# Post norms by column sums, shift products inside their wait, the last additions on TensorE, and five smaller reorderings, in a 512-token transformer stack

## What is computed

```python
# block 1
x = x + mixed @ w_out              # mixed: gated mLSTM branch and gated differential attention branch
x = x + ffn_conv(rmsnorm(x))       # up 1024->2*2816, conv over 3 tokens, gelu gate, down
x = x + sigmoid(rmsnorm(x) @ w_ple_gate) * (p @ w_ple)
# block 2: two layers
x = x + (stick_breaking(...) * silu(gate)) @ w_out
x = x + (mla(...)            * silu(gate)) @ w_out      # 8 heads, 4 query blocks of 128 each
# block 3
for sub in (swiglu, hybrid_mixer, swiglu):              # each with shift, scale, gate from w_ada
    h = sub(rms_norm(x, g_pre) * (1 + scale) + shift)
    x = x + c * (1 + gate) * rms_norm(h, g_post)        # the POST NORM of this document; c = 0.5, 1, 0.5
# hybrid_mixer holds the forgetting ("FoX") attention: 8 heads, logits = q k / 8 + cum[q] - cum[k]
```

## Time and profile before

| | |
|---|---|
| median of 3 runs | 2669.25 us (2667.76 to 2672.13) |
| the profiled execution | 2670.79 us, of which the span is 2669.0 us |
| TensorE busy | 2469.7 us, 93% of the span |
| VectorE, ScalarE, GpSimd busy | 51%, 38%, 38% |
| mean granted TensorE clock | 0.964 |
| HBM traffic | 242.06 MB read, 91 GB/s over the span |

### The profile page before, as it was taken

How to read it: one execution, slowest core, us unless ns; L and a number is a source line. 1 busy time by engine, 2 the same in 40 slices (tenths; PEclk the granted TensorE clock), 3 DMA queues, 4 the chain that set the end, 5 groups by cost and what they waited for, 6 DMA issues and landing times.

```text
span 2669.0 us, 31132 instructions
## 1 busy us (share of the span) xinstructions
PE 2469.7 (93%) x11612; PEld 1976.9 (74%) x11612; DVE 1362.1 (51%) x1883; ACT 1022.4 (38%) x1320; POOL 1013.0 (38%) x758
## 2 busy tenths in 40 slices
PE   6999799899998999998988899999979997899996
PEld 5887677688887778676766678888859655688885
DVE  6456567866667561444447652222373535522225
ACT  4444476422223444665456442222242433322221
POOL 3332244455444443122433244444424104344442
PEclk8999899999999999999999899999989998999998
DMA  3220497222222121111221122222222001122221
GB/s 135 80 79 32 166 359 271 103 95 94 95 98 90 68 91 64 48 48 48 91 83 64 48 79 95 94 94 94 94 69 94 32 17 63 63 95 99 102 98 47
DMA packets 35812, 245.50 MB, mean 92 GB/s; under 512 B 3935, under 2 KB 3935, under 8 KB 7044
## 3 DMA queue, kind: packets, MB, share of 16 engines
q1 hardware_dynamic: 29952, 207.12, 21.7%
q10 hardware_dynamic: 5764, 37.06, 3.7%
HBM read 242.06 MB, written 2.11 MB: 91 GB/s over the span
## 4 chain that ended last, share of the span: by engine, by line
issue 56%; POOL 27%; PE 14%; DVE 2%; DVEq 1%; POOLq 0%; ACT 0%; ACTq 0%
POOL WL L280 27%; PE PS L310 5%; PE PS L312 5%; PE PS L311 5%; DVE ARENA L2350 0%; DVE X L2355 0%; DVE ARENA L1683 0%; POOLq L284 0%; DVEq L2354 0%; DVE ARENA L1701 0%; DVEq L2031 0%; DVE ARENA L1708 0%; DVEq L1724 0%; PE PS L372 0%; POOLq L277 0%
## 5 line engine op out<-in xcount | busy, mean ns | idle before, releaser
L280 POOL TENSOR_TENSOR WL<-WT,WH 128x512 fp32r<-128x512 f32 x754 | 1012.8, 1374 | 1617.0 <-ACT WH L1012 1097.7
L310 PE MATMUL PS<-HH,WH 128*128 128x512 f32 x1568 | 623.5, 398 | 30.7 <-DVE HL L1717 8.8
L312 PE MATMUL PS<-HH,WL 128*128 128x512 f32 x1568 | 615.8, 393 | 0.0
L311 PE MATMUL PS<-HL,WH 128*128 128x512 f32 x1568 | 615.6, 393 | 0.0
L1334 ACT CAST WH<-WT 128x2048 fp32r<-128x2048 f32 x90 | 172.1, 1912 | 604.1 <-PE PS L310 604.1
L310 PEld LDWEIGHTS PS<-HH,WH 128*128 128x128 f32 x1568 | 297.6, 190 | 109.3 <-DVE HL L1717 14.2
L310 PE MATMUL PS<-YH,WH 128*128 128x512 f32 x840 | 337.4, 402 | 41.5 <-POOL WL L280 8.7
L312 PEld LDWEIGHTS PS<-HH,WL 128*128 128x128 f32 x1568 | 297.4, 190 | 63.2
L311 PEld LDWEIGHTS PS<-HL,WH 128*128 128x128 f32 x1568 | 297.9, 190 | 59.6 <-issue 0.3
L311 PE MATMUL PS<-YL,WH 128*128 128x512 f32 x840 | 332.2, 395 | 0.0
L312 PE MATMUL PS<-YH,WL 128*128 128x512 f32 x840 | 332.2, 395 | 0.0
(11 more groups left out here) (290 smaller groups left out, 3354.2 us busy)
## 6 DMA issues: line engine op xcount, KB each, us to landing
WT<-weights SPq DMA_DIRECT2D x188, 1024.0 KB, 4.9
ARENA<-w_ada ACTq DMA_DIRECT2D x33, 1024.0 KB, 7.3
ARENA<-w_ada SPq DMA_DIRECT2D x3, 1024.0 KB, 7.6
X<-x_fm SPq DMA_DIRECT2D x4, 512.0 KB, 8.0
out_fm<-X SPq DMA_DIRECT2D x8, 256.0 KB, 2.0
ARENA<-rel_rows ACTq DMA_DIRECT2D x1, 1024.0 KB, 5.2
CON<-constants SPq DMA_DIRECT2D x1, 704.0 KB, 10.1
WT<-weights SPq DMA_DIRECT2D x1, 512.0 KB, 5.5
```

Source lines behind the costliest of these rows:

```text
L280: i = nc.gpsimd.tensor_tensor(WL[s][:, e], WT[s][:, e], WH[s][:, e].bitcast(F32), ALU.subtract)
L310: i0 = nc.tensor.matmul(o, w[0], r[0], start=first, stop=False, skip_group_check=True)
L311: nc.tensor.matmul(o, w[0], r[1], start=False, stop=False, skip_group_check=True)
L312: i2 = nc.tensor.matmul(o, w[1], r[0], start=False, stop=last, skip_group_check=True)
```

## The change

1. **Post norms.** `norm_sum(two_parts)` is replaced by `post_sum`: the sum over features is taken with the squares as the stationary operand and one column of ones as the moving one, so it comes out as 128 x 4 (token within a block on the partition, block in the column). DVE adds up only the squares 0 to 4; the parts 5, 6 and 7 go to TensorE one by one. ACT's root and DVE's reciprocal are then of 128 x 4 elements. DVE writes four diagonal blocks (identity times factor, 128 x 512) and one float32 matmul with ONES spreads them over the partitions in bank 5, from where L2350's successor reads the factor.
2. **Inside the wait.** The next panel's first shift products stand between the column sums and that matmul. ACT casts the next panel right behind the root instead of after the third tile of `raw_after_post`. Eight matmuls of no use (`keep_warm`) stand ahead of the raw tile. A `sqrt_ahead` (a function table load) stands ahead of the squares in both later FFNs.
3. **Last post norm.** X[0] to X[4] are added on TensorE: identity times X[k], then identity times the scaled ACC[k], both float32 in one bank; ACT copies the sum to X[k]. DVE adds 5 to 7 as before.
4. **Merge.** The sum for the last head of differential attention stands behind the first tile of panel `G_MERGE`; SP loads panel `G_MERGE + 2` ahead of the wait for `da_done`.
5. **FFN1's end.** ACT's copies of PLE tiles 0, 1, 2 stand behind the raw tiles 5, 6, 7.
6. **MLA.** `OUT3_STEPS` goes; the first output panel is computed whole after the last tile.
7. **FoX.** The decay is added by one matmul of 128 rows: the high part in rows 0 to 7, the low part in rows 32 to 39 of `LBH`, the stationary operand picks both.

```diff
-            def norm_sum(second=False, two_parts=False):
+            def post_sum(bank, meanwhile):
                 n["sq"] += DT
-                n["acc"] += DT - 2 if two_parts else DT - 1
+                n["acc"] += POST_ACC
...
+                for k in range(POST_ACC, DT):
+                    if k > POST_ACC:
+                        pe.wait_ge(sem("sq_ready"), n["sq"] - DT + k + 1)
+                    part = SQ[:, (k - 1) % 3, :] if k > POST_ACC else ACC1
+                    for t in range(NQ):
+                        m = nc.tensor.matmul(PS[:, bank + t, 0:1], part[:, P * t:P * (t + 1)], ONES[:, 0:1], start=k == POST_ACC,
+                                             stop=k == DT - 1, skip_group_check=True)
+                m.then_inc(sem("ms_ready"), 1)
+                meanwhile()
+                pe.wait_ge(sem("diag_ready"), n["post"])
+                nc.tensor.matmul(psb(5), ONES, NRS, start=True, stop=True).then_inc(sem("nrow_ready"), 1)
...
-            norm_sum(two_parts=True)
+            post_sum(2, lambda: shift_ahead(G_FFN3, 2))
             ffn(G_FFN3, sums="tiles", shift=2)
-            norm_sum(two_parts=True)
...
+            post_sum(0, lambda: (last_add(0, X), last_add(1, X)))
+            for k in range(LAST):
+                if k + 2 < LAST:
+                    last_add(k + 2, X)
+                pe.wait_ge(sem("last_norm"), k + 1)
+                last_add(k, ACC)
...
+            def post_root(bank):
+                act.wait_ge(sem("ms_ready"), n["ms"])
+                f(COLS[:, 40:44], PS[:, bank:bank + NQ, 0], ACT.Sqrt, scale=1.0 / D, bias=par("eps")).then_inc(sem("root_ready"), 1)
...
+            def post_factor():
...
+                nc.vector.reciprocal(COLS[:, 44:48], COLS[:, 40:44])
+                dve.drain()
+                tt(NRS.rearrange("p (t n) -> p t n", t=NQ), IDENT.unsqueeze(1).to_broadcast([P, NQ, P]),
+                   COLS[:, 44:48].unsqueeze(2).to_broadcast([P, NQ, P]), ALU.mult).then_inc(sem("diag_ready"), 1)
...
-                        stt(out=NT[:, k % 3, :], in0=ACC[:, k, :], scalar=mod(s, 2)(k), in1=NRS, op0=ALU.mult, op1=ALU.mult)
+                        stt(out=NT[:, k % 3, :], in0=ACC[:, k, :], scalar=mod(s, 2)(k), in1=psb(5), op0=ALU.mult, op1=ALU.mult)
...
-            stream(2, G_MERGE + 2)
+            stream(2, G_MERGE + 3)
             sp.wait_ge(sem("da_done"), 1)
...
-            da_squares(DA_HEADS - 1)
+            open_panel(G_MERGE)
+            feature_tiles(G_MERGE, G_MERGE % 2, 8, 256, h_hi, h_lo, (0,))
+            pe.wait_ge(sem("dsq_ready"), DA_HEADS)
+            nc.tensor.matmul(psb(2), ONES, SQB_, start=True, stop=True).then_inc(sem("dsum_ready"), 1)
+            feature_tiles(G_MERGE, G_MERGE % 2, 8, 256, h_hi, h_lo, (P,), first_of_panel=False)
...
-                one = CONR[0:8, COFF["ident"] + w:COFF["ident"] + w + 1].to_broadcast([8, P])
-                for part in (LBH, LBL):
-                    nc.tensor.matmul(o, one, part[0:8, k], start=False, stop=False, skip_group_check=True)
+                nc.tensor.matmul(o, LBH[:, S + w:S + w + 1].to_broadcast([P, P]), LBH[:, k], start=False, stop=False,
+                                 skip_group_check=True)
...
                 if conv:
-                    raw(lambda k: par("norm_ple", k))
+                    for k in range(DT):
+                        raw(lambda k: par("norm_ple", k), k, k + 1)
+                        if k >= 5:
+                            embed(k - 5)
```

More of the change, by code:

```diff
@@ L368, in norm_sum @@
                 pe.wait_ge(sem("sq_acc"), n["acc"])
[L369 to L372 removed]
+                m = nc.tensor.matmul(psb(3), ONES, ACC1, start=True, stop=True)
                 m.then_inc(sem("ms_ready"), 1)
@@ L434, in out_gemm, with keep_warm @@
                         i2.then_inc(sem("a_done"), 1)
+            def keep_warm(o, count):
+                for _ in range(count):
+                    nc.tensor.matmul(o, IDENT_R, CONR[:, 0:S], start=True, stop=True, skip_group_check=True)
             def out_step(g, src, ready, c, b, k):
@@ L1735, in trail @@
                     raw_lo(k, gain, dst)
[L1736 removed]
+                if gain or k <= POST_ACC:
                     accumulate(k)
```

165 lines of the change are left out of this document (99 added, 66 removed).

## The result

The changed kernel takes 2635.91 us (median of four runs, 2633.1 to 2638.14) beside 2670.69 for the kernel before (four runs, 2667.76 to 2674.76): a ratio of 0.9865, 95% interval 0.9851 to 0.9879. 35 us are gone.

A forecast was written before the change was run, and what follows sets the result against it. TensorE, busy 93% of the span, was taken as the bound, so removed matmuls or idle time count. Terms 4.5 + 8.4 + 4.5 + 4.0 + 5.0 + 7.5 = 33.9 us off 2670.79 give 2636.9, 2635 beside the median; range 2625 to 2648.

The forecast's parts named there:

- A: Rival: clock and GpSimd overlap decide, the post norms gain 1 us instead of 12.9, giving 2647 us; chance 0.12.
- B: Rival: merge and MLA reorderings only move holes, gaining 1 us instead of 9.5, giving 2644 us; chance 0.13.
- D: Rival: FoX's granted clock falls to 1.2 GHz and the kernel is slower, 2745 us at half clock throughout; chance 0.03.
- FoX, 7.5 predicted: FoX's decay: one matmul fewer per tile, mean 0.24 us over 32 tiles, 7.5 us saved after some waits.
- Merge, 4.5 predicted: Merge stage: third panel ready near 315 us instead of 318.53, perhaps fewer slow matmuls; 4.5 us saved, between 0 and 6.
- which is 3.1 later: Merge stage: ACT waits for `CROW` only, which comes 3.1 us later, so the third panel's cast starts at 307.4.
- FFN1's end, 4.0 predicted: End of FFN1: earlier copies move the chain of copies, cast and GpSimd's pieces by 4.0 us, at least 2.
- MLA, 5 predicted: MLA's output: steps leave the tiles, two holes and nine half-clock matmuls go; 5 us saved, between 0 and 9.
- The two post norms, 4.2 each predicted: After FFN2 and the mixer: 2.4 us from an earlier factor plus 1.8 from GpSimd's overlap, each between 1.5 and 6.
- the column sums of the last part are four matmuls ... so 0.96: Post norms: behind the last square only four column-sum matmuls remain, taking 0.96 us.
- sixteen shift products ... 1.9 us: Post norms after FFN2 and mixer: sixteen shift products behind the sums take 1.9 us, little longer than root, reciprocal and diagonals.
- The tail, 4.5 predicted: Last post norm: 0.4 + 1.5 + 3.2 = 5.1 us from earlier square, factor and additions on TensorE; taken as 4.5.

The follow-up runs named there:

- MLA undone: Changed kernel with the first panel of MLA's output product again in six steps inside the last attention tiles: 2638.06 us, ratio 0.9861.
- one part alone: Changed kernel with column sums of the last part only, 4 matmuls instead of 16 in each of three post norms (computes another norm): 2630.96 us, ratio 0.9837.
- the one with four tiles: Four feature tiles instead of five added on TensorE at the end, on top of the split shift products: 2630.01 us, ratio 0.9851.
- the run with the split products: Changed kernel with only the first pair of shift products ahead of the spreading matmul, seven pairs behind, no useless matmuls: 2631.02 us, ratio 0.9838.

## Why the prediction was right, and where its terms were off

The forecast was 2635.0 in a range of 2625 to 2648; it is 2635.91. None of the rivals came in. A (the post norms give back): they gave 3.7, 2.7 and 4.3 us, and in the tail the granted clock was back at 1.00 from 2622.15 on, where the eight later additions run. B (holes only move): merge gave 5.6 and MLA 3.5. D (FoX falls to half clock): the granted clock is 1.00 from FoX's first score to its last, and the stage is 9.4 us shorter. But the sum is right partly by luck: some terms came out larger and some smaller than predicted, and 1.9 of the 34.8 us between the profiles lie where nothing was changed.

- **FoX, 7.5 predicted, 9.4 found.** The step counted the removed matmul alone. Its price was right (0.21 us between two starts); missing was that the mask's matmul behind it takes 0.06 instead of 0.16 in the changed kernel. The estimate of 4.4 us from the Trainium skill (TensorE: Matmul & The Clock Gate, Back-to-back issue gap; there the formula is that of an isolated matmul), which the prediction weighed, is less than half of it.
- **Merge, 4.5 predicted, 5.6 found** (4.0 to 8.6 by the stage's scatter). "That part gives 0.8 only and leaves a new hole" is borne out as far as the scatter lets one see: with the sum back, nothing changes beyond it. The third panel started at 311.56 with 1.2 us of waiting, not at 315. The chain is the forecast one (ACT waits for `CROW`, idle 5.4 us, then casts), but `CROW` is there by 303.5, so the cast starts at 304.5 and not at 307.4. The step that failed is "which is 3.1 later": in the kernel before ACT didn't wait for `CROW`, it came to it 1.7 us after its landing (303.33, landed 301.68), so 1.7 of the delay were slack, and 1.0 more had been won ahead of the stage. Of the 7 us earlier start that same 1.0 was there before the stage and some was paid back in waits for `WL` of 1.1 to 2.8 us at later panels.
- **FFN1's end, 4.0 predicted, 3.7 found**, confirmed by undoing it (hole of 5.77 us back).
- **MLA, 5 predicted, 3.5 found.** "In the middle" between all and nothing hidden was too hopeful: of 9.5 us of matmuls 6.4 had been hiding latency. They now show as waits of 1.2 to 1.6 us.
- **The two post norms, 4.2 each predicted, 3.7 and 2.7 found, and mostly not where the prediction put them.** It gave 2.4 us to an earlier factor and 1.8 to GpSimd's overlap. The factor gave 1.0 after FFN2 (first scaling behind MLA's last transposition, 429.1 us before and 428.1 with MLA undone) and took 0.3 in the mixer (69.2 us behind FoX's last score, before 68.9); the loop gave 2.7 and 2.6, and in the mixer 0.5 more lies between the loop's last scaling and the last eviction. From the last square to the first scaling "4.0 to 5.0 us" were forecast, and 7.8 and 7.1 were found. The steps that failed: first, "the column sums of the last part are four matmuls ... so 0.96". All sixteen queue behind the down product and end 2.1 to 2.5 us after the last square, as running one part alone showed. Second, "sixteen shift products ... 1.9 us": after FFN2 they took 3.4 us, 0.21 for each of the records, at 1.2 GHz, and held the spreading back by 2.0 us; putting fourteen of them behind it (and leaving out the useless matmuls) gave 2.4 to 3.2 us after FFN2 and 0.7 to 3.4 in the mixer. Their count was right; the clock was not, as it had fallen inside the sums in front. Third, "against 7.4 us": that is the tail's own distance, and in the mixer it was 6.4 before. GpSimd's overlap was taken too low: one addition is slowed instead of four instructions. That the two misses went opposite ways and left each place near its forecast is luck.
- **The tail, 4.5 predicted, 4.3 found**, its parts partly off: from the first scaling to the last copy 7.7 us instead of the 8.8 forecast, as a wide addition costs 0.86 us from start to start and not 0.96, but the stores cost 2.0 us more than before and not 1.0. From square to scaling it is 6.3 us, forecast 5.9, and 8.1 where the clock falls early. As the runs split it, 2.5 come without any addition on TensorE, from the factor and DVE's tighter rounds. With five tiles on TensorE the tail is 19.9 to 20.0 us where the clock falls late and 21.7 where it falls early, as in seven of ten profiles (20.7 in the one with four tiles); without them it is 21.7, with an early fall. So at the same early fall five tiles on TensorE give nothing, and of the 1.8 us of the late ones some 0.9 are the sums' own.
- **The useless matmuls** cost nothing in their place: after FFN2 they end 2.3 us ahead of the raw tile. Nor do they show in the clock: around this post norm it was granted at 0.50 for 13.7 us with them (1925.8 to 1936.1 and 1939.5 to 1942.9), and for 13.7 without them in the run with the split products. Neither they nor the new `sqrt_ahead` were taken out alone.

## What to carry to other kernels

Work that is pulled into a wait is free only if it ends before the thing waited for: compare its length at the clock that the wait itself will bring, and put just the piece that frees a buffer in front. A sum over parts on TensorE counts all its parts if the engine is still busy when the early ones could run. When one matmul is removed, read the spacing of the next one too. Read a chain in each place where it stands: the same post norm took 8.1, 6.4 and 7.4 us from square to scaling in one kernel. And look at what runs beside a moved operand: here the loops, with their factor in PSUM and not in SBUF, lost less time beside GpSimd, and that gave more than the chain that was meant to be shortened.

## What was not expected of the hardware

- A record of a matmul with one moving column takes 0.11 us at full clock (32 in 3.63 us), one with two columns 0.21 at half; the granted clock fell from 1.00 to 0.50 in the middle of such a row of matmuls, with TensorE busy all the time.
- The 128 x 128 mask product took 0.16 us until the next start behind a product with 8 rows and 0.06 behind one with 128 (0.11 where that one had 128 columns).
- Beside GpSimd's pieces a DVE addition of two SBUF operands took 1.59 instead of 0.69, `L1751` with `X` and `HH` 0.90 instead of 0.75, and a scaling with one operand in PSUM the same 0.75. The Trainium skill (SBUF — State Buffer, Who interferes with whom) says that a DVE instruction with at most one SBUF input, outside the 2-port perf modes, doesn't contend with GpSimd, while one with two SBUF inputs contends with a GpSimd instruction that reads SBUF; these rows agree, the one with `X` and `HH` by 0.15 us only.
- Stages of the same code differ from one profile to the next: the merge stage took 223.2 to 227.8 us; its waits for GpSimd, of some 1 to 3 us, are not the same ones in each profile.
